# Seven block products for the q, k and v tiles of a hybrid SSD and DeltaNet block on one Trainium2 core

## The chip, the cores and the metric

The kernel is one launch on one core of a Trainium2 chip. The metric is the device time of that core in microseconds, the median of several executions of the same program. Engines are named as in the profile: PE is TensorE (PEld its weight loads), DVE is VectorE, ACT is ScalarE, POOL is GpSimd, SP is SyncE, which here only issues transfers.

## The reference, cut to what matters

Sequence and model width are both 1024, batch and depth 1, everything in float32.

```
h = rms_norm(x, g_mix_pre)
proj = h @ w_in                                  # 1024 x 1024 by 1024 x 8736
z, xbc, dt_raw, qkv, gate, b_raw, a_raw, m_gate = split(proj)
xbc = silu(causal_dwconv(xbc, conv_ssm_w) + conv_ssm_b)       # 1536 channels, 4 taps
qkv = silu(causal_dwconv(qkv, conv_gdn_w))                    # 3072 channels, 4 taps
y_ssm, y_gdn = chunked scans over xs, B, C and over q, k, v   # z and gate enter as silu(.)
x = x + rms_norm((gate_ssm * (y_ssm @ w_br_ssm) + gate_gdn * (y_gdn @ w_br_gdn)) @ w_out)
x = x + rms_norm((gelu(causal_dwconv(h @ w_ffn_gate) + b) * (h @ w_ffn_up)) @ w_ffn_down)
x = x + rms_norm(sigmoid(x @ w_ple_gate) * (p @ w_ple_proj))
```

The change concerns the products for `xbc` and `qkv` with their convolutions, and the stage behind them.

## The kernel before, in words

**Numbers in two parts.** Every matrix product is made of three in the fast float32 format of TensorE: a value is split in a high part (`act_hi`, `w_hi`) and the rest (`act_lo`, `w_lo`), and a product is hi x hi + lo x hi + hi x lo. The activations `h` lie on chip, channels on partitions: 8 blocks of 128 channels (`KD`) by 1024 tokens.

**Tiles.** A tile is 128 output channels by 1024 tokens. `pe_unit` (L488) makes a plain tile with `pe_steps` (L470): 8 blocks of input channels, two halves of 512 tokens, three matmuls each, so 48 matmuls of 128x512 into one of four PSUM buffers of two banks. A buffer is taken with `wait_buffer` and given back through `tile_free`. SP loads weights by 1 MB blocks of two tiles into one of two slots of `w_raw` (`load_block`, L428), GpSimd splits each tile's weights with two instructions of 128x1024 (`split_unit`, L465 and L467) into one of two slots of `w_hi` and `w_lo`; `unit_begun` tells it that TensorE has begun the unit before.

**The x, B, C, q, k and v tiles** (70 to 462 us) are 12 `ssm` tiles and 24 `gdn` tiles, in the order of the list `PROJ` (L370). For each, VectorE copies PSUM to `xin` (L2938), makes the first tap (L2945) and three more taps (L2951) into `ring_a`; ScalarE applies Silu into `ring_b` and sends the tile to the scratch tensor `spill` (L2856, L2859). Between tiles lie the head factors: `head_softplus` (L524) behind the twelfth tile, the transposes for `O_TM` behind the q and k tiles, the sums over tokens for `O_CUM` behind the first four v tiles, with `tm_sources`, `tm_sums` and four exponentials. Loops over four tiles (`run_tiles`) are hardware loops except for the first four tiles.

**The gates' stage** (462 to 731 us, functions with `_a`) makes 16 plain tiles for `z` and `gate` in 128 steps of six matmuls, in two PSUM buffers. Between the steps that `A_START` (L1152) and `A_AT` name, TensorE does the small work of the eight chunks of 128 tokens of the DeltaNet branch: `sums` (the sums of squares), `v_rows`, `gram` and `k_rows` in the other two buffers. For each chunk SP loads q, k and v back from `spill` (`qkv_load`, L1348), two broadcast decay arrays (`decays_load`, L1340) and a weight block, and stores seven results (`stores`, L1353). ScalarE makes squares, norms and exponentials (L1227 to L1245) and evicts the gate tiles (`evict`, L1218); VectorE scales q and k (L1290, L1292) and forms the matrices (L1300 to L1305), and from chunk 4 on solves blocks by substitution (`substitute`, L1402). GpSimd splits weights and prepares the decays (L1329, L1331).

**The FFN stage** (up to 2080 us) already makes a pair of tiles by seven block products (Strassen's scheme in Winograd's form): the 1024x1024 activations and the 1024x256 weights are cut in two by two blocks. Four sums of weight blocks come from VectorE (`sums`, L2404, L2416), the high parts from ScalarE (L2108), the low parts from GpSimd (L1755). A product (`product`, L1845) is 12 matmuls into one PSUM bank. ScalarE copies the first product out of PSUM (L2115) and VectorE adds up the two tiles with seven evictions (`evict`, L2418, L2434). The four sums of activation blocks are made once, with their high and low parts (L2397, L2078, L2402). There is one semaphore order for all engines, written out by hand.

## Time and profile before

| | |
|---|---|
| three runs, us | 2559.57, 2562.78, 2572.18 (median 2562.78) |
| the profiled execution, us | 2576.11 |
| its span, us | 2574.3 |
| busy us PE, PEld, DVE, ACT, POOL | 2468.0, 2041.2, 1542.1, 723.0, 1179.6 |
| mean granted clock of TensorE | 0.985 |

The span is the time from the first to the last instruction of the profiled execution. Busy times add up the instructions of an engine; a matmul's recorded length is longer than the distance to the next one, because matmuls are pipelined. A wait names the instruction whose end released the waiting engine.

### The profile page before, as it was taken

What the parts mean: (1) busy time and instruction counts of PE and PEld (TensorE: products, weight loads), DVE (VectorE), ACT (ScalarE), POOL (GpSimd) and SP (SyncE); (2) the same over time, 40 slices, a digit from 0 to 9 for tenths busy, and PEclk for the clock granted to TensorE, in tenths of its full rate; (3) what the DMA queues carried; (4) which work ended last, traced back from release to release, by engine and by line L of the source; (5) the groups of instructions that cost most, each with busy time, mean ns of one, the idle gap of its engine ahead of it and who ended that gap; (6) DMA issues with size and microseconds to landing.
All of it is one profiled execution on the core that took longest, in us unless ns stands there. A gap on an engine that the chain in (4) does not pass through costs nothing. (4 is left out here: it accounts for less than half of the span.)

```text
span 2574.3 us, 30045 instructions
## 1 busy us (share of the span) xinstructions
PE 2468.0 (96%) x11684; PEld 2041.2 (79%) x11684; DVE 1542.1 (60%) x1359; ACT 723.0 (28%) x830; POOL 1179.6 (46%) x631
## 2 busy tenths in 40 slices
PE   6999999999899999989999799999999999999998
PEld 5888888777678888878878578888888878888786
DVE  4679776435774667654243796776776752322585
ACT  4100101355412223232003353333333331000332
POOL 1333333456444545443334355655566543333563
PEclk7999999999999999999999899999999999999999
DMA  5222322688775756646232212222221253122332
GB/s 197 103 98 83 113 90 100 173 269 273 245 242 142 207 167 186 190 126 214 98 143 89 95 50 83 85 86 73 98 80 66 98 196 115 49 82 82 119 112 105
DMA packets 293583, 336.28 MB, mean 131 GB/s; under 512 B 44445, under 2 KB 250602, under 8 KB 289386
## 3 DMA queue, kind: packets, MB, share of 16 engines
q1 hardware_dynamic: 260634, 272.47, 33.2%
q10 hardware_dynamic: 32848, 62.40, 6.5%
q8 instruction: 71, 1.16, 0.2%
q14 instruction: 30, 0.25, 0.0%
HBM read 231.55 MB, written 103.28 MB: 130 GB/s over the span
## 5 line engine op out<-in xcount | busy, mean ns | idle before, releaser
L480 PE MATMUL ps<-act_hi,w_hi 128*128 128x512 f32 x1712 | 682.4, 399 | 14.8 <-POOL w_lo L467 4.5
L484 PE MATMUL ps<-act_hi,w_lo 128*128 128x512 f32 x1712 | 667.5, 390 | 0.0
L483 PE MATMUL ps<-act_lo,w_hi 128*128 128x512 f32 x1712 | 667.0, 390 | 0.0
L465 POOL TENSOR_SCALAR w_hi<-w_raw 128x1024 fp32r<-128x1024 f32 x151 | 171.7, 1137 | 914.8 <-issue 603.8
L467 POOL TENSOR_TENSOR w_lo<-w_raw,w_hi 128x1024 fp32r<-128x1024 f32 x151 | 409.2, 2710 | 12.6
L480 PEld LDWEIGHTS ps<-act_hi,w_hi 128*128 128x128 f32 x1712 | 322.2, 188 | 87.6 <-issue 11.6
L483 PEld LDWEIGHTS ps<-act_lo,w_hi 128*128 128x128 f32 x1712 | 322.3, 188 | 67.6 <-issue 3.6
L484 PEld LDWEIGHTS ps<-act_hi,w_lo 128*128 128x128 f32 x1712 | 321.8, 188 | 67.6
L1755 POOL TENSOR_TENSOR w_lo<-sm,w_hi 128x512 fp32r<-128x512 f32 x120 | 208.6, 1740 | 108.7 <-ACT w_hi L2108 108.7
L1755 POOL TENSOR_TENSOR w_lo<-w_raw,w_hi 128x512 fp32r<-128x512 f32 x90 | 138.8, 1543 | 164.5 <-ACT w_hi L2108 164.5
L2951 DVE SCALAR_TENSOR_TENSOR ring_a<-xin,par,ring_a 128x1024 f32<-128x1024 f32 x108 | 185.0, 1713 | 11.8 <-DVE ring_a L2945 0.3
L1870 PE MATMUL ps<-t,w_hi 128*128 128x512 f32 x480 | 186.8, 389 | 0.0
L1871 PE MATMUL ps<-t,w_hi 128*128 128x512 f32 x480 | 186.8, 389 | 0.0
L1872 PE MATMUL ps<-t,w_lo 128*128 128x512 f32 x480 | 186.7, 389 | 0.0
L1870 PE MATMUL ps<-act_hi,w_hi 128*128 128x512 f32 x360 | 140.9, 391 | 4.6 <-POOL w_lo L1755 4.6
L1872 PE MATMUL ps<-act_hi,w_lo 128*128 128x512 f32 x360 | 140.7, 391 | 0.0
L1871 PE MATMUL ps<-act_lo,w_hi 128*128 128x512 f32 x360 | 140.6, 391 | 0.0
L2856 ACT ACTIVATE ring_b<-ring_a 128x1024 f32<-128x1024 f32 x36 | 38.2, 1061 | 330.9 <-DVE ring_a L2951 330.9
L2517 DVE TENSOR_TENSOR tile<-ps,tile 128x1024 f32<-128x1024 f32 x24 | 29.4, 1224 | 160.8 <-PE ps L484 133.8
L2108 ACT ACTIVATE w_hi<-sm 128x512 fp32r<-128x512 f32 x120 | 75.4, 630 | 135.9 <-PE ps L1872 135.9
L1781 PE MATMUL ps<-act_hi,w_hi 128*128 128x512 f32 x256 | 103.1, 403 | 10.8 <-DVE act_lo L2360 7.1
L1870 PEld LDWEIGHTS ps<-t,w_hi 128*128 128x128 f32 x480 | 90.1, 188 | 18.8
(348 smaller groups left out, 4137.0 us busy)
## 6 DMA issues: line engine op xcount, KB each, us to landing
w_raw<-in_w_in_dram SPq DMA_DIRECT2D x34, 1024.0 KB, 5.2
spill<-ring_b ACTq DMA_DIRECT2D x67, 512.0 KB, 2.7
w_raw<-in_w_ffn_down_dram SPq DMA_DIRECT2D x18, 1024.0 KB, 4.8
w_raw<-in_w_ffn_up_dram SPq DMA_DIRECT2D x16, 1024.0 KB, 5.1
w_raw<-in_w_ffn_gate_dram SPq DMA_DIRECT2D x16, 1024.0 KB, 5.1
f_cm<-ring SPq DMA_DIRECT2D x32, 512.0 KB, 2.6
qkv_a<-spill SPq DMA_DIRECT2D x8, 1536.0 KB, 8.3
dec_a<-cum_rows SPq DMA_DIRECT2D x16, 512.0 KB, 14.3
```

The costliest lines, as they stand in the source:

```text
L465: nc.gpsimd.tensor_scalar(hi, raw, 1.0, 0.0, ALU.mult, ALU.add).then_inc(split_done, 1)
L467: nc.gpsimd.tensor_tensor(lo, raw, hi.bitcast(f32), ALU.subtract).then_inc(split_done, 1)
L480: first = nc.tensor.matmul(o, wh, mov[0][:, k, c], start=(k == 0), stop=False)
L483: nc.tensor.matmul(o, wh, mov[1][:, k, c], start=False, stop=False)
L484: last = nc.tensor.matmul(o, wl, mov[0][:, k, c], start=False, stop=(k == KD - 1))
L1755: nc.gpsimd.tensor_tensor(product_slot(w_lo, j), product_in(q, i), product_slot(w_hi, j).bitcast(f32), ALU.subtract).then_inc(w_low[0], 1)
L1781: first = nc.tensor.matmul(dst, wh, mov[0][:, k, in_half(half)], start=(k == 0), stop=False)
L1870: nc.tensor.matmul(dst, wh[:, k, :], mh[:, k, :], start=(k == 0), stop=False)
L1871: nc.tensor.matmul(dst, wh[:, k, :], ml[:, k, :], start=False, stop=False)
L1872: last = nc.tensor.matmul(dst, wl[:, k, :], mh[:, k, :], start=False, stop=(k == 3))
L2108: a(product_slot(w_hi, j), product_in(q, i), ACT.Copy).then_inc(w_high[0], 1)
L2951: v.scalar_tensor_tensor(out=ring_a[:, slot, :], in0=xin[:, slot, tap:tap + SEQ], scalar=col_of(wname, tap * nt + t0 + n), in1=ring_a[:, s ...
```

## The change

The 24 q, k and v tiles are made in twelve pairs by the seven block products of the FFN stage: `sp_pairs`, `pool_pairs`, `pe_pairs`, `act_pairs`, `dve_pairs` and `dve_sums` are new and written out, and `run_tiles` with its hardware loops is gone. VectorE makes the four weight sums of every pair. The four activation sums (`ct1` to `ct4`) are made by VectorE and ScalarE during the first twelve tiles. In all 36 tiles ScalarE makes the first tap, out of PSUM for the first twelve and from the assembled tile in the pairs, and Silu writes in place; the other three taps of the first twelve read PSUM, and the copy to `xin` is gone (`xin` and `ring_b` hold the assembled tiles of the pairs). The head work moves to between the first twelve tiles, and the eleven copies to `tmc` move with it. In the gates' stage `A_START` changes, SP's block requests move behind the loads of the chunk, and ScalarE's evictions move. GpSimd splits the first gate unit after the last pair's products. The diff, cut to its core:

```diff
-    A_START = [15, 27, 40, 55, 70, 85, 100, 116]
+    A_START = [22, 33, 45, 58, 72, 86, 101, 116]
...
+    IN_PRODUCTS = ("a11", "a12", "s1", "s2", "s4", "s3", "a22")
+    SUM_AT = {"s1": (0, 1), "s3": (3, 2), "s2": (1, 3), "s4": (2, 4)}
+    C_EVICT = {0: (1, 0), 1: (3, 0), 2: (2, 0), 3: (4, 0), 4: (5, 1), 5: (2, 1), 6: (6, 1)}
...
+    def pool_pairs(pool):
+        for p in range(C_PAIRS):
+            for i in range(PRODUCTS):
+                j = PRODUCTS * p + i
+                past(pool, c_high, j + 1)
+                nc.gpsimd.tensor_tensor(c_slot(w_lo, j), c_product_in(p, i), c_slot(w_hi, j).bitcast(f32),
+                                        ALU.subtract).then_inc(c_low[0], 1)
...
+    def pe_pairs(pe):
...
+        for p in range(C_PAIRS):
+            for i in range(PRODUCTS):
+                j = PRODUCTS * p + i
+                past(pe, c_low, j + 1)
...
+                elif p % 2:
+                    if i == 0 and p > 1:
+                        past(pe, c_copied, p - 1)
+                    if i == 1:
+                        past(pe, c_copied, p)
+                    if i in (2, 3):
+                        past(pe, c_evicted, SUMMED * (p - 1) + (1, 6)[i - 2])
+                elif i in (0, 1, 5):
+                    past(pe, c_evicted, SUMMED * (p - 1) + {0: 1, 1: 6, 5: 7}[i])
...
+                for k in range(4):
+                    first = nc.tensor.matmul(dst, wh[:, k, :], mh[:, k, :], start=(k == 0), stop=False)
...
+                    nc.tensor.matmul(dst, wh[:, k, :], ml[:, k, :], start=False, stop=False)
+                    last = nc.tensor.matmul(dst, wl[:, k, :], mh[:, k, :], start=False, stop=(k == 3))
+                last.then_inc(c_prod[0], 1)
+        pe.sem_inc(unit_begun, QKV_T - 1)
...
+        def first_tap(t):
+            past(act, c_evicted, SUMMED * (t // 2) + (4, 7)[t % 2])
+            act_first_tap(act, J_Q + t, c_tile(t), pcol("conv_gdn_w", 3 * QKV_T + t), None)
...
+        for p in range(C_PAIRS):
+            for i in range(PRODUCTS):
+                if p or i > 1:
+                    c_high_of(act, p, i)
+                if p and i == 0:
+                    first_tap(2 * p - 2)
+                if i == 3:
+                    copy(p)
+                    if p == 0:
+                        xbc_out(act, XBC_T - 1)
+                    if p > 1:
+                        silu(2 * p - 3)
+                if p and i == 4:
+                    first_tap(2 * p - 1)
+                if p and i == 6:
+                    silu(2 * p - 2)
...
+        for p in range(C_PAIRS):
+            evicts(p, (0,))
+            if p:
+                taps(2 * p - 2)
+            evicts(p, (1, 2))
+            if p < C_PAIRS - 1:
+                dve_sums(dve, p + 1)
+            evicts(p, (3, 4, 5))
+            if p:
+                taps(2 * p - 1)
+            evicts(p, (6,))
+        taps(QKV_T - 2)
+        taps(QKV_T - 1)
...
-        for m in range(2):
-            split_unit(pool, U_A, m)
+        past(pool, c_prod, PRODUCTS * C_PAIRS - 2)
+        pool.sem_inc(split_done, 2 * QKV_T)
+        split_unit(pool, U_A, 0)
+        past(pool, c_prod, PRODUCTS * C_PAIRS)
+        split_unit(pool, U_A, 1)
...
         for c in range(NCH):
-            if c:
-                block_load(c + 1)
             if c < NCH - 1:
                 decays_load(c + 1)
                 qkv_load(c + 1)
+            block_load(c + 2)
             if c == 4:
                 blocks_load(0)
-            if c == NCH - 1:
-                block_load(NCH + 1)
             stores(c)
...
+        after_norms = {0: 2, 2: 5, 5: 10, 6: 12, 7: 14}
+        after_decays = {1: 4, 3: 7, 4: 9}
+        after_squares = {0: 3, 2: 6, 3: 8, 5: 11, 6: 13, 7: 15}
...
+        conv(0)
+        head_softplus(dve, lambda step: conv({5: 1, 11: 2}[step]) if step in (5, 11) else None)
+        conv(3)
...
+        conv(10)
+        sum_low(ct4, ct4_raw, 4)
+        dve_sums(dve, 0)
+        conv(11)
+        dve_pairs(dve)
```

## Rows read from the trace of the kernel before

**Rows 1.** The header of the page.

```profile
span 2574.3 us, 30045 instructions
```

**Rows 2.** Stretches: length, busy us (instructions) of PE, PEld, DVE, ACT, POOL; PEclk, DMA, GB/s.

```profile
70.00:462.00 392.00, 392.00 (x1744) 323.49 (x1743) 301.24 (x199) 44.90 (x42) 137.11 (x70) 1.00 0.27 96
462.00:731.00 269.00, 257.04 (x1130) 202.75 (x1129) 132.53 (x143) 133.46 (x120) 140.91 (x68) 0.99 0.79 249
...
1600.00:1800.00 200.00, 200.00 (x884) 165.60 (x883) 139.78 (x147) 76.16 (x108) 120.05 (x75) 1.00 0.23 79
```

**Rows 3.** Timeline of TensorE near the end of the v tiles: start, us, instruction.

```profile
440.02 0.39 PE L480 MATMUL ps<-act_hi,w_hi 128*128 128x512 f32 x1
...
450.22 0.39 PE L480 MATMUL ps<-act_hi,w_hi 128*128 128x512 f32 x1
```

**Rows 4.** Waits of TensorE in the gates' stage: us in total, times, longest.

```profile
PE ps L1190 <- DVE hrow L1292: 7.3, 2, 5.4
PE ps L480 <- POOL w_lo L467: 2.6, 2, 1.3
PE ps L1170 <- ACT hrow L1232: 2.0, 1, 2.0
```

**Rows 5.** Groups of VectorE in the FFN stage: busy us, mean ns, idle before.

```profile
L2416 DVE TENSOR_TENSOR sm<-w_raw 128x512 f32<-128x512 f32 x54 | 49.1, 949 | 19.1 <-POOL w_lo L1755 19.1
L2447 DVE SCALAR_TENSOR_TENSOR fa<-xinb,par,fa 128x1024 f32<-128x1024 f32 x26 | 43.8, 1685 | 1.8
...
L2434 DVE TENSOR_TENSOR ring<-ps,sx 128x512 f32<-128x512 f32 x52 | 35.9, 691 | 19.6 <-PE ps L1872 18.3
...
L2416 DVE TENSOR_TENSOR sm<-sm,w_raw 128x512 f32<-128x512 f32 x27 | 32.7, 1210 | 0.0
```

**Rows 6.** Timelines of VectorE (160 us; FFN stage) and of GpSimd (FFN stage).

```profile
162.28 4.14 DVE L2951 SCALAR_TENSOR_TENSOR ring_a<-xin,par,ring_a 128x1024 f32<-128x1024 f32 x3
...
1679.78 3.50 DVE L2447 SCALAR_TENSOR_TENSOR fa<-xin,par,fa 128x1024 f32<-128x1024 f32 x2
...
1666.36 1.28 POOL L1755 TENSOR_TENSOR w_lo<-sm,w_hi 128x512 fp32r<-128x512 f32 x1 [0.89 <-ACT w_hi L2108]
...
1679.96 2.24 POOL L1755 TENSOR_TENSOR w_lo<-sm,w_hi 128x512 fp32r<-128x512 f32 x1 [0.81 <-ACT w_hi L2108]
```

**Rows 7.** A group of ScalarE in the FFN stage.

```profile
L2091 ACT ACTIVATE fa<-xinb,par 128x1024 f32<-128x1024 f32 x13 | 16.2, 1246 | 2.9 <-DVE xinb L2434 2.8
```

**Rows 8.** Groups of VectorE, 60 to 480 us; of line 2397 in the tail: min/median/max ns.

```profile
L2951 DVE SCALAR_TENSOR_TENSOR ring_a<-xin,par,ring_a 128x1024 f32<-128x1024 f32 x108 | 185.0, 1713 | 11.8 <-DVE ring_a L2945 0.3 <-DVE ring_a L2951 0.3
L2945 DVE TENSOR_SCALAR ring_a<-xin,par 128x1024 f32<-128x1024 f32 x36 | 48.2, 1338 | 6.7 <-DVE xin L2938 6.1 <-DVEq L2941 0.2
L2938 DVE COPY xin<-ps 128x1024 f32<-128x1024 f32 x36 | 44.0, 1222 | 78.9 <-PE ps L484 70.3 <-PE ps L2705 8.4 <-DVE hrow L546 0.2
...
L2397 DVE TENSOR_TENSOR t_raw<-res x2: 2282/2283/2284, 1483.0 to 1487.5; 128x2048 f32<-128x2048 f32 x2
```

**Rows 9.** Timeline of GpSimd at a split; of TensorE at 1064 us; a stretch after.

```profile
473.24 1.05 POOL L465 TENSOR_SCALAR w_hi<-w_raw 128x1024 fp32r<-128x1024 f32 x1 [6.99 <-issue]
474.37 2.39 POOL L467 TENSOR_TENSOR w_lo<-w_raw,w_hi 128x1024 fp32r<-128x1024 f32 x1
...
1063.97 1.97 PE L924 MATMUL ps<-ident,qs 128*128 128x128 f32 x8 [3.37 <-DVE qs L1126]
...
1065.00:1070.00 5.00, 5.00 (x30) 4.54 (x29) 5.00 (x5) 1.55 (x2) 0.68 (x1) 0.76 0.69 166
```

**Rows 10.** Timelines of ScalarE and TensorE in the gates' stage; landings of line 1351.

```profile
507.25 2.01 ACT L1232 ACTIVATE hrow<-qkv_a 128x1024 f32<-128x1024 f32 x2 [4.39 <-DMA qkv_a<-spill]
...
509.56 3.59 PE L1170 MATMUL ps<-hrow,ones 128*128 128x512 f32 x8
...
680.02 6.22 PE L1190 MATMUL ps<-hrow 128*128 128x256 f32 x16 [5.35 <-DVE hrow L1292]
...
DMA to landing us min/median/max: 7.0/8.3/13.7
```

More of the change, by code:

```diff
@@ L388, in uses_spilled @@
         return 16 * len(range(slot, j_end, 2))
-    def run_tiles(eng, tiles, j0, body):
-        if j0 == 0:
-            for n in range(tiles):
-                body(None, n)
-        else:
-            with eng.Fori(0, tiles // 4) as it:
-                for n in range(4):
-                    body(it, n)
     def uses(o0, n, it=None, per=0):
@@ L531, in then @@
             dve.wait_ge(head_dve, step[0])
+            between(step[0])
         dve.wait_ge(head_act, 2)
@@ L2622, in _ @@
             sp.dma_start(d_ch[64 * half:64 * half + 64, :], v.broadcast_to([64, KD]), allow_slow_non_contiguous=True).then_inc(d_in, 16)
[L2623 to L2629 removed]
+        for n in range(2, XBC_T, 2):
+            load_block(sp, w_in_k[:, :, COL_XBC + P * n:COL_XBC + P * n + 2 * P], 1, n // 2)
+        sp_pairs(sp)
         sp_a(sp)
@@ L2654, in _ @@
         split_unit(pool, U_SMALL, 0)
-        for kind, col, tiles, j0, o0 in PROJ:
-            run_tiles(pool, tiles, j0, lambda it, n: split_unit(pool, 1 + j0, n, it, 4))
+        for n in range(XBC_T):
+            split_unit(pool, 1, n)
+        pool_pairs(pool)
         pool_a(pool)
@@ L2871, in _ @@
+        act_pairs(act)
         act_a(act)
@@ new lines, in conv @@
+        def conv(n):
+            past(dve, c_first, n + 1)
+            o = xbc_use(n)
+            b, c = uses(o, 0)
+            src, out = buf(b), ring_a[:, n % 2, :]
+            for i, back in enumerate((1, 2, 3)):
+                if i:
+                    dve.wait_ge(conv_step, 2 * n + i)
+                v.scalar_tensor_tensor(out=out[:, back:SEQ], in0=src[:, 0:SEQ - back], scalar=pcol("conv_ssm_w", (3 - back) * XBC_T + n),
+                                       in1=out[:, back:SEQ], op0=ALU.mult, op1=ALU.add
+                                       ).then_inc(conv_step if i < 2 else tile_free[b], 1)
+            if n == 0:
+                dve.wait_ge(tile_free[b], c + 1)
+                v.sem_inc(tile_free[b], UNUSED[b])
@@ new lines, in _ @@
+        raw_op(ct2_raw, ct2_raw[:, :, :], ct1_raw[:, :, :], ALU.subtract)
+        conv(5)
+        past(dve, c_traw, 5)
+        sum_low(ct1, ct1_raw, 1)
+        conv(6)
+        tm_sums(dve)
+        conv(7)
+        dve.wait_ge(tm_act, 4)
+        for at, i, row, n in TM_COLS:
+            v.tensor_copy(tmc[:, :, at:at + n], tmh[:, :, i, row:row + n]).then_inc(tm_kept, 1)
+        dve.wait_ge(tm_kept, len(TM_COLS))
+        dve.wait_ge(cum_kept, 16)
+        raw_op(ct3_raw, ct2_raw[:, :, :], part(act_hi, 0, 0), ALU.subtract)
```

407 lines of the change are left out of this document (277 added, 130 removed).

## The prediction

> **What bounds the kernel now.** Read the header of the page first: the span is 2574.3 us [rows 1]. Then the busy time by stretch. From 70 to 462 us, the stage that this change rewrites, TensorE is busy in all 392.00 us at full granted clock, VectorE in 301 us and GpSimd in 137 us; in the gates' stage (462 to 731 us) TensorE idles 12 us; in the FFN stage, which runs seven block products for each pair of tiles already, it is busy in all of 200 us with VectorE at 140 us [rows 2]. A busy TensorE is worth its instruction rate: from the timeline, 45 matmuls start between 440.02 and 450.22 us, one each 0.2267 us [rows 3]. So a plain tile (48 matmuls) takes 10.88 us and 24 q, k and v tiles take 261.1 us. The path is TensorE, and fewer matmuls shorten it only if nothing else becomes the slower engine. The waits of TensorE in the gates' stage are few: 7.3 us on VectorE before `gram`, 2.6 us on GpSimd's weight split, 2.0 us on ScalarE's squares [rows 4].
>
> **Fewer matmuls.** A pair takes 7 products of 12 matmuls, 84 instead of 96, at 0.2267 us: 19.04 us a pair, 228.5 us for twelve. That is 144 matmuls less: **-32.6 us**, certain as work, not as time.
>
> **VectorE in a pair.** It now does 7 evictions of 128x512 out of PSUM, 4 weight sums of 128x512 and 6 filter taps of 128x1024 in each 19.04 us. By the means of the FFN stage [rows 5]: 7 x 0.69 = 4.8; sums 2 x 0.949 + 1.210 + about 1.2 = 4.3; 6 x 1.685 = 10.1; together 19.2 us, and some 0.04 us between each two of 17 instructions makes 19.9. That is already more than TensorE's 19.04. The FFN stage does two pairs with 14 evictions, 8 sums, 4 taps and 2 products in 38 us and has 30% of VectorE free; here a pair has three times the taps, and nothing is free. Those means hide a contention. Three taps alone take 4.14 us (1.38 each), but two taps beside a GpSimd instruction take 3.50 us, and the GpSimd instruction that needs 1.28 us by itself takes 2.24 us when it begins 0.18 us after a tap [rows 6]: GpSimd ends about 1.15 us after the tap did, and the second tap 1.1 us after GpSimd. The two take turns. A PSUM eviction keeps its 0.69 us. Bounds: with no turn lost VectorE needs 7 x 0.72 + 4 x 0.62 + 6 x 1.38 = 15.9 us (sums at 0.62 by the undisturbed ones, an estimate from 0.69 less the start-up shared by two in a row), so TensorE's 19.04 sets the pair; with all seven GpSimd subtractions of a pair in VectorE's way it needs 15.9 + 7 x 1.15 = 24.0 us. A busy VectorE spends a quarter of its time in evictions, which collide with nothing, so 5 of 7 collide, at 0.9 us each (part of a start-up is hidden): 15.9 + 4.5 = **20.4 us a pair**, nearest to the row sum of 19.9. Where it shows: VectorE's fourth eviction of a pair completes an early tile, ScalarE's first tap waits for it, ScalarE's copy of the next pair's second weight block stands behind that tap in its queue, GpSimd's subtraction behind that, and TensorE's second product of the next pair waits, 1.4 us per pair. The first two pairs run on the lead that exists. So 10 x 1.36 = **+13.6 us** given back (0 to +30; at the full 24.0 the change loses).
>
> The shared port is also a rule of the Trainium skill: "SBUF — State Buffer", section "SBUF: two separate sides", says that a VectorE instruction with two SBUF inputs and a GpSimd instruction exclude each other for a whole instruction, the loser waiting fully. By it the taps and sums (6 x 1.1 + 4 x 0.55 us) and the subtractions (7 x 1.15 us) hold the port 16.9 us of a 19.04 us pair, so the port alone does not bound the pair; rows 6 agree with the turns it describes.
>
> **ScalarE and GpSimd in a pair.** ScalarE: two first taps of 1.25 us [rows 7], eight copies of half that size at half that, two Silu at no more than 1.25: 10 us of 19.04. GpSimd: 7 subtractions of 1.3 to 1.7, at most 12 us. Both are hidden, and so are the 1 MB block loads, requested a pair ahead as in the FFN stage. If VectorE's lag grows, the cover of ScalarE's 1.25 us tap is what goes first.
>
> **The first twelve tiles.** VectorE loses the 1.22 us PSUM copy and the 1.34 us first tap of each [rows 8], and its taps now read PSUM with one SBUF input, so about 3.8 us a tile instead of 7.7. It gains nine 128x2048 sums and differences of the activations and four more for their low parts, 13 x 2.3 = 30 us [rows 8]. The head work, which stood partly among the q, k and v tiles, is 301 us less 36 tiles of 1.22 + 1.34 + 3 x 1.71 = 7.7 us [rows 2, 8], so 24 us. With 46 us of taps and 4 us of weight sums VectorE has 104 us of work beside 130 us of TensorE. Its queue order has about 2.5 us of room where tile 6 and tile 7 need their buffers back. I take **+1 us** (0 to +6). The transposes and cumulative sums on TensorE only change places.
>
> **From pairs to gates.** GpSimd may split the first gate unit only after the products of the last pair, because it waits for `unit_begun` to reach 37 and TensorE adds the missing 23 after its last product. The split is 1.05 + 2.39 us [rows 9] and stood during a tile before; VectorE's overdue taps can stretch it by two turns of about 1.1. TensorE stands still 3.5 us (2.9 to 5.5). After a stop of 3.37 us the granted clock fell below 2.4 GHz: 0.76 over the next 5 us [rows 9], 0.24 x 5 = 1.2 us lost. **+5 us** in all.
>
> **The gates' stage.** `A_START[0]` goes from step 15 to 22 (a step is 6 matmuls, 1.36 us): the last tiles finish later (VectorE has up to three tiles' taps left, 12 us; then Silu, store and a 1.5 MB load of about 9 us), some 26 us against 22 x 1.36 = 29.9 us. The 2.0 us wait on the squares goes. SP's block request moves from ahead of the decay and q/k/v loads to behind them and ahead of the stores of the preceding chunk: weights arrive a chunk earlier, so the two GpSimd waits (2.6 us) go. Behind it in SP's queue stand seven stores; its own wait, for the split of the chunk's units, is met by then. The q/k/v load no longer has the decay loads in front. But the next chunk's sums start one step sooner for chunks 1 and 2, and there was no room: the load let the squares run from 507.25 to 509.26 us, and the sums began at 509.56 [rows 10]. I take back 1 us. The 5.35 us stop before `gram` at 680.02 [rows 10] stays: the steps from `k_rows(5)` to `gram(6)` are 12 as before, and VectorE's substitution fills them. Sum: -2.0 - 2.6 + 1 + 0.6 for chunk 5, which begins a step sooner after chunk 4: **-3 us** (-11, all stops gone, to +8).
>
> Sum: -32.6 + 13.6 + 1 + 5 - 3 = **-16.0 us**. The profiled execution took 2576.1 us (span and 1.8 us around it), 13.3 us above the median of 2562.8; both should move alike, to 2560 and **2547 us**.
>
> **Rivals.**
> 1. Full cover: VectorE's turns fall into its evictions, a pair takes 19.04 us. For: the FFN stage shows no TensorE stop at all. Against: 19.9 us by its own means. 2562.8 - 29.6 = 2533 us.
> 2. VectorE bound harder: a spill that lands late holds ScalarE's second tap too, or the stops drop the clock. A pair of 21.6 us adds 12 us: 2559 us, no measurable change.
> 3. Slower than before: the 1 MB block that SP now requests beside each 1.5 MB q/k/v load delays it. The landings of that load lie between 7.0 and 13.7 us, median 8.3 [rows 10]; 13.7 for seven chunks is 7 x 5.4 = 38 us with no room to hide it: 2547 + 38 = 2585 us. It decides from 16 / 7 = 2.3 us a chunk on. Against: the block is requested after the load.
> That the change does not do what it says is excluded for the matmuls, which are written out.
>
> **Numbers.** Forecast case 0.42 (its own range 2540 to 2555), rival 1 0.22, rival 2 0.26, rival 3 0.10. A measurement here tells about 0.5%, 12.8 us, from no change. Faster by more than that (under 2550.0): all of rival 1, three quarters of the forecast, little of rival 2, 0.53. Within it: the rest of both and nearly all of rival 2, 0.38. Slower: most of rival 3, 0.09. The range leaves out only rival 3 and the far end of rival 1: 2527 to 2567 us.
>
> **What would show it.** A pair of products about 20.4 us long, with a wait of TensorE on GpSimd's subtraction near 1.4 us at the second product, and VectorE over 95% busy from the third pair on. Taps near 1.8 us in the pairs and 1.25 us on PSUM. One stop of 3 to 5 us between pairs and gates, with a dip of the clock. No wait on the weight split inside the gates' stage, and the 5 us stop before `gram` of chunk 6 still there. Wrong if VectorE has clear idle time in the pairs, or if sums in the gates' stage wait on q/k/v loads.

## The result, and the profile after

| | median us | runs | lowest to highest | profiled execution, span |
|---|---|---|---|---|
| before | 2570.74 | 12 | 2559.57 to 2577.61 | 2576.11, 2574.3 |
| after | 2577.33 | 12 | 2571.73 to 2580.71 | 2578.95, 2577.2 |

The ratio is 1.003 with an interval of 1.0016 to 1.0045: some 7 us slower, within the 0.5% that the prediction called no change, where 16 us less was forecast. The prediction started from three runs of the kernel before (median 2562.78); twelve runs have 2570.74, so 8 us of the distance to its 2547 us lie in that starting point and not in the change. First, the stretches of the kernel after, as in [rows 2]: the first line ends where the pairs end, the second is the gates' stage, the third the FFN stage, whose cost did not change.

```profile
70.00:433.00 363.00, 359.83 (x1590) 293.73 (x1589) 330.74 (x278) 143.17 (x174) 185.71 (x105) 1.00 0.29 100
433.00:726.00 293.00, 260.66 (x1093) 202.06 (x1092) 128.56 (x137) 129.56 (x118) 132.29 (x67) 0.94 0.71 223
1600.00:1800.00 200.00, 200.00 (x884) 165.62 (x883) 138.90 (x146) 76.07 (x107) 118.43 (x73) 1.00 0.24 83
```

The pairs paid: TensorE comes to the gates' units at 432.55 us, where it came at about 461.8 before (its first sums fell due at step 15 at 482.2 us, less 15 x 1.36). That is 29 us ahead. The last store of the gates' stage is requested at 726.32 us, before at 723.09. So this stage went from 261.3 to 293.8 us: **32 us lost where 3 were to be gained**. TensorE idles 32 us in it, against 12, and the granted clock is 0.94 in place of 0.99: some 20 us of the loss are idle time, and the other 12 fit the lower clock (0.05 of 293 us is 15 us, an estimate). The waits of TensorE in that stretch (us in total, times, longest) stand against [rows 4]; a stop, below, is one such wait:

```profile
PE ps L1414 <- ACT hrow L1478: 13.2, 4, 4.0
PE ps L494 <- POOL w_lo L481: 11.1, 2, 7.9
PE ps L1434 <- DVE hrow L1539: 7.9, 2, 4.3
```

The first line is the sums waiting for the squares (2.0 us before), the second the split of gate weights (2.6 us before, forecast to go), the third `gram`. In the pairs, VectorE's groups from 225 to 425 us (busy us, mean ns, idle before):

```profile
L719 DVE SCALAR_TENSOR_TENSOR ring_a<-xin,par,ring_a 128x1023 f32<-128x1023 f32 (+2 forms) x33 | 57.8, 1751 | 0.8
L719 DVE SCALAR_TENSOR_TENSOR ring_a<-ring_b,par,ring_a 128x1023 f32<-128x1023 f32 (+2 forms) x30 | 52.1, 1737 | 0.7
L692 DVE TENSOR_TENSOR csm<-w_raw 128x512 f32<-128x512 f32 x20 | 31.8, 1630 | 0.0
L711 DVE TENSOR_TENSOR ring_b<-ps,csx 128x512 f32<-128x512 f32 x21 | 14.4, 684 | 5.1 <-PE ps L599 4.7
```

VectorE is busy in 197.47 of those 200 us: it bounds the pairs, as forecast (e4 below tests it). And the timeline of TensorE gives the length of a pair, from the second product of one to the second product of the next, 377.07 - 357.55 = 19.52 us:

```profile
357.55 0.50 PE L595 MATMUL ps<-act_hi,w_hi 128*128 128x512 f32 x1 [0.17 <-POOL w_lo L563]
377.07 0.50 PE L595 MATMUL ps<-act_hi,w_hi 128*128 128x512 f32 x1 [0.18 <-POOL w_lo L563]
```

**Where the gates' stage lost it.** The timeline at its head, chunk 0 (ScalarE's squares, TensorE's sums, GpSimd, then the stop):

```profile
464.57 2.00 ACT L1478 ACTIVATE hrow<-qkv_a 128x1024 f32<-128x1024 f32 x2 [8.96 <-DMA qkv_a<-spill]
465.88 5.37 PE L1414 MATMUL ps<-hrow,ones 128*128 128x512 f32 x8 [3.23 <-ACT hrow L1478]
...
469.33 1.89 POOL L1579 TENSOR_TENSOR dec_a<-dec_a,tmc 128x1024 f32<-128x1024 f32 x1 [20.11 <-issue]
...
473.66 1.06 POOL L479 TENSOR_SCALAR w_hi<-w_raw 128x1024 fp32r<-128x1024 f32 x1
...
474.80 2.34 POOL L481 TENSOR_TENSOR w_lo<-w_raw,w_hi 128x1024 fp32r<-128x1024 f32 x1
...
477.29 0.77 PE L494 MATMUL ps<-act_hi,w_hi 128*128 128x512 f32 x1 [3.29 <-POOL w_lo L481]
...
479.98 1.37 PE L1422 MATMUL ps<-ident,qkv_a 128*128 128x128 f32 x8
```

GpSimd stood still 20.11 us in front of the decay work of chunk 0, and the split of unit `U_A+3` stood behind that in its queue. The unit is due at step 24. With the first sums at step 22 that is between the sums and the v rows (`L1422`), so the stop of 3.29 us delays the chunk too; with the sums at step 15 the v rows were already done. The sums themselves and the matmuls behind the stop ran at a lower clock: 5.37 us for the sums that took 3.59 us in [rows 10], and 0.77 us for a matmul of 0.39 us, which is the lower of the clock's two levels (1.2 and 2.4 GHz). Next, SyncE's requests and GpSimd's split of the block that came next:

```profile
487.75 0.36 SPq L1606 DMA_DIRECT2D qkv_a<-spill  x1
488.16 4.07 SPq L451 DMA_DIRECT2D w_raw<-in_w_in_dram  x1
```

```profile
498.63 1.04 POOL L479 TENSOR_SCALAR w_hi<-w_raw 128x1024 fp32r<-128x1024 f32 x1 [11.99 <-DMA w_raw<-in_w_in_dram]
...
502.25 0.77 PE L494 MATMUL ps<-act_hi,w_hi 128*128 128x512 f32 x1 [7.85 <-POOL w_lo L481]
```

Block 2 went out behind the second q, k and v load, 33 us behind the first, and TensorE needed it at 494.4 us.

**The view that explains the stage is the chain of its chunks.** The q, k and v load of chunk c+1 overwrites what VectorE reads last in chunk c (`L1539`). So a chunk is: load, squares, sums, norms, v rows, VectorE's last read, next load; eight of them in a row. A period is the time from one load's request to the next. From the timelines of SyncE, the request of the first and the eighth such load and of the last store of the stage (us), with each kernel's ratio to before:

| kernel | load 0 | load 7 | seven periods | last store | ratio, interval |
|---|---|---|---|---|---|
| before | 473.98 | 680.00 | 206.0 | 723.09 | 1 |
| after | 454.67 | 685.46 | 230.8 | 726.32 | 1.0030, 1.0016 to 1.0045 |
| e3 | 461.54 | 675.33 | 213.8 | 716.22 | 0.9989, 0.9974 to 1.0003 |
| e2 | 454.62 | 670.98 | 216.4 | 713.83 | 0.9969, 0.9953 to 0.9986 |
| e14 | 454.92 | 669.11 | 214.2 | 710.99 | 0.9962, 0.9949 to 0.9974 |
| e15 | 454.95 | 667.30 | 212.4 | 709.19 | 0.9956, 0.9939 to 0.9972 |
| e4 | 441.00 | 667.85 | 226.9 | 709.72 | 0.9954, 0.9940 to 0.9968 |
| e7 | 462.51 | 671.73 | 209.2 | 713.79 | 0.9949, 0.9934 to 0.9964 |
| e5 | 455.09 | 658.45 | 203.4 | 699.65 | 0.9938, 0.9914 to 0.9962 |
| e19 | 452.73 | 663.70 | 211.0 | 706.76 | 0.9934, 0.9916 to 0.9952 |
| e16 | 455.26 | 658.49 | 203.2 | 698.58 | 0.9923, 0.9907 to 0.9940 |
| e13 | 455.98 | 655.74 | 199.8 | 697.87 | 0.9916, 0.9888 to 0.9943 |
| e18 | 452.02 | 653.47 | 201.4 | 697.52 | 0.9911, 0.9894 to 0.9928 |
| e17 | 452.22 | 656.34 | 204.1 | 696.91 | 0.9908, 0.9887 to 0.9928 |
| e20 | 453.89 | 654.79 | 200.9 | 696.07 | 0.9898, 0.9881 to 0.9915 |
| e12 | 441.43 | 651.19 | 209.8 | 694.62 | 0.9878, 0.9848 to 0.9909 |

From the eighth load to the last store it is 40.1 to 44.1 us in every one, so the stage ends when the chain ends. TensorE's steps are links of the chain too: its sums and v rows stand behind the gate units that come first in its order. In the kernel before, the sums waited for the squares in chunk 0 alone (2.05 us), but there was little room: in chunks 1 to 6 they began 1.9 to 5.2 us behind the start of the squares, and 1.3 us is the least in any chunk (507.25 and 509.56 us in chunk 1, [rows 10]). Steps and chain were of nearly one length. In the kernel after, the sums waited for the squares in chunks 0, 3, 4 and 5, and `gram` for VectorE in chunks 5 and 6. After the change TensorE arrives 29 us sooner, the chain only 19 us (454.67 against 473.98), and then five of the seven periods took longer: 33.1, 34.8, 25.2, 30.2, 31.8, 39.2, 36.5 us after, against 25.6, 26.4, 25.9, 32.5, 29.4, 31.4, 34.8 before.

### The profile page after: what moved, and what is told of

Same layout as the page of the kernel before. It is cut to its first block and busy times, and to the rows that moved or that the text cites. A ratio compares the mean times of both kernels' runs of the same rounds, so it can differ in the third digit from the quotient of the medians.

```text
span 2577.2 us, 29644 instructions
## 1 busy us (share of the span) xinstructions
PE 2451.5 (95%) x11540; PEld 2019.9 (78%) x11540; DVE 1567.1 (61%) x1432; ACT 819.0 (32%) x961; POOL 1225.2 (48%) x667
## 5 line engine op out<-in xcount | busy, mean ns | idle before, releaser
L494 PE MATMUL ps<-act_hi,w_hi 128*128 128x512 f32 x1328 | 533.6, 402 | 24.7 <-POOL w_lo L481 13.0
L498 PE MATMUL ps<-act_hi,w_lo 128*128 128x512 f32 x1328 | 519.7, 391 | 0.0
L497 PE MATMUL ps<-act_lo,w_hi 128*128 128x512 f32 x1328 | 519.2, 391 | 0.0
L479 POOL TENSOR_SCALAR w_hi<-w_raw 128x1024 fp32r<-128x1024 f32 x127 | 146.2, 1151 | 752.6 <-issue 630.7
L481 POOL TENSOR_TENSOR w_lo<-w_raw,w_hi 128x1024 fp32r<-128x1024 f32 x127 | 343.2, 2702 | 10.6
L494 PEld LDWEIGHTS ps<-act_hi,w_hi 128*128 128x128 f32 x1328 | 250.7, 189 | 84.1 <-issue 19.9
L498 PEld LDWEIGHTS ps<-act_hi,w_lo 128*128 128x128 f32 x1328 | 250.5, 189 | 53.2
L497 PEld LDWEIGHTS ps<-act_lo,w_hi 128*128 128x128 f32 x1328 | 250.9, 189 | 52.2 <-issue 3.3
L2111 PE MATMUL ps<-act_hi,w_hi 128*128 128x512 f32 x360 | 141.2, 392 | 4.2 <-POOL w_lo L1996 4.2
L2112 PE MATMUL ps<-act_lo,w_hi 128*128 128x512 f32 x360 | 141.0, 392 | 0.0
L2113 PE MATMUL ps<-act_hi,w_lo 128*128 128x512 f32 x360 | 141.0, 392 | 0.0
L2758 DVE TENSOR_TENSOR tile<-ps,tile 128x1024 f32<-128x1024 f32 x24 | 29.4, 1224 | 160.8 <-PE ps L498 133.8
L2022 PE MATMUL ps<-act_hi,w_hi 128*128 128x512 f32 x256 | 103.1, 403 | 10.4 <-DVE act_lo L2601 6.8
L2423 ACT ACTIVATE act_hi<-f_raw 128x1024 fp32r<-128x1024 f32 x32 | 31.2, 1047 | 254.9 <-DMA f_raw<-f_cm 254.9
L563 POOL TENSOR_TENSOR w_lo<-csm,w_hi 128x512 fp32r<-128x512 f32 x48 | 84.7, 1774 | 43.4 <-ACT w_hi L631 43.4
```

Of the source, the lines that this page charges most:

```text
L479: nc.gpsimd.tensor_scalar(hi, raw, 1.0, 0.0, ALU.mult, ALU.add).then_inc(split_done, 1)
L481: nc.gpsimd.tensor_tensor(lo, raw, hi.bitcast(f32), ALU.subtract).then_inc(split_done, 1)
L494: first = nc.tensor.matmul(o, wh, mov[0][:, k, c], start=(k == 0), stop=False)
L497: nc.tensor.matmul(o, wh, mov[1][:, k, c], start=False, stop=False)
L498: last = nc.tensor.matmul(o, wl, mov[0][:, k, c], start=False, stop=(k == KD - 1))
L563: nc.gpsimd.tensor_tensor(c_slot(w_lo, j), c_product_in(p, i), c_slot(w_hi, j).bitcast(f32), ALU.subtract).then_inc(c_low[0], 1)
```

## The experiments

Diffs are against the kernel named; a us figure between two of them is the difference of their ratios times 2571. An interval reaches 3 to 8 us to either side, so where two overlap the text says so. Three theories at first: A, the chain starts late because the last tiles do; B, requests at the head of the stage are late; C, the re-ordering itself.

**e3, two requests early.** The load of block 2 is then left out of the loop's first turn.

```diff
+        past(sp, c_prod, PRODUCTS * C_PAIRS)
+        decays_load(0)
+        block_load(2)
         for k in range(2):
             sp.wait_ge(spilled[k], uses_spilled(J_Z, k))
         qkv_load(0)
-        decays_load(0)
```

> The change, with two of SP's requests at the head of the gates' stage moved: decays_load(0) and block_load(2) go out as soon as the last pair product is done (about 433 us), ahead of the waits for the last spills. After the change they were requested at 455.1 and 488.2 us. Theory B (the lost time of the gates' stage comes from late requests at its head): ScalarE's copy and GpSimd's half of unit U_A+3 no longer stand behind a late decay load, so TensorE's stop of 3.29 us at 477.29 goes, and block 2 is there 50 us sooner, so the stop of 7.85 us at 502.25 goes, and with them some of the lost clock (0.93 and less in the slices after them): 11 to 16 us less than the change, 2561 to 2566 us. Theory A (the chain of chunks starts late because VectorE and ScalarE finish the last q, k and v tiles late): the two stops go, but TensorE then runs into the next waits for squares and gram sooner, so that most of it comes back as longer stops at 562, 594, 626 and 649 us: under 4 us gained.

Both stops on the split went, and the kernel took 10 us less than the change: nearer to B, a little short of its 11 to 16. But a new stop of 5.92 us came at 460.37 us, on ScalarE's eviction of a gate tile, and the first q, k and v load went out 7 us later. ScalarE's first tap of tile 23 waits for the spill of tile 21; beside the early loads that spill took 12.90 us. The timeline of ScalarE in e3, and the same wait in the kernel after:

```profile
439.76 0.33 ACTq L617 DMA_DIRECT2D spill<-ring_a  x1
452.64 1.15 ACT L608 ACTIVATE ring_a<-ring_b,par 128x1024 f32<-128x1024 f32 x1 [12.90 <-DMA spill<-ring_a]
```

```profile
442.51 1.15 ACT L608 ACTIVATE ring_a<-ring_b,par 128x1024 f32<-128x1024 f32 x1 [2.73 <-DMA spill<-ring_a]
```

A store of 0.5 MB on the critical chain lost 10 us to a weight block and decay rows that could have waited. In e7, which has the same early requests, the wait was 12.02 us.

**e4, no VectorE backlog.**

```diff
-  v.scalar_tensor_tensor(out=out[:, back:SEQ], in0=src[:, 0:SEQ - back], ..., in1=out[:, back:SEQ], ...)
+  v.scalar_tensor_tensor(out=out[:, back:back + 16], in0=src[:, 0:16], ..., in1=out[:, back:back + 16], ...)
```

> The change, with VectorE's three filter taps of each of the 24 q, k and v tiles done for the first 16 tokens only (the filters of these tiles are left out beyond that; 72 instructions shrink from about 1.5 us to 0.1 us). VectorE loses about 100 us of work in the pairs' stage and has nothing overdue at its end. Theory A (late last tiles start the chunk chain late): Silu of tile 23 comes at about 437 instead of 450 us, the first q, k and v load at about 441 instead of 454.7, the wait of the first sums for squares (3.23 us at 465.9) goes, and the later chunks have 10 us more room, so the waits for squares and gram in the gates' stage fall from 21 us to under 8, 12 us or more gained there; the pairs take 19.04 us instead of 19.5, 5 us more. In all 2555 to 2562 us. Theory B (late requests of the decays and of block 2, and the order of the eight chunks): the chain starts sooner, but block 2 still goes out behind the second q, k and v load and lands late, and the sums and grams from chunk 3 on wait as before: 5 us from the pairs and 3 us from the first sums, about 2569 us.

19.5 us less than the change, 2560.69 us, in A's range. Twelve pairs took 228.5 us (201.5 to 430.0), 19.04 each, with no wait on `L563` at all: VectorE was the bound. The first load went out at 441.00. But 25 us of waits stayed in the gates' stage, 18 of them for squares and before `gram`, not under 8, and its seven periods were nearly as bad as the change's (226.9 us against 230.8). So lateness and slow periods are two losses.

**e5, the gates' stage as before.** SyncE's order (the block of the next units a chunk later, behind the stores of the chunk before), the start steps and ScalarE's order of evictions are those of the kernel before; the short form of the edit:

```diff
-    A_START = [22, 33, 45, 58, 72, 86, 101, 116]
+    A_START = [15, 27, 40, 55, 70, 85, 100, 116]
...
+            if c:
+                block_load(c + 1)
             if c < NCH - 1:
                 decays_load(c + 1)
                 qkv_load(c + 1)
-            block_load(c + 2)
```

> The twelve pairs stay as in the change, but the gates' stage is put back: SP's order of requests, A_START and ScalarE's order of evictions are those of the kernel before. Theory C (the re-ordering itself costs the gates' stage its 32 us): the stage falls back to about 260 us after the pairs, and the kernel takes about 2545 to 2550 us. Theory A (the chain of chunks starts late against TensorE, 9 us later than before, whatever the order): the first sums, now at step 15, wait about 10 us for the first load and its squares, and nothing is gained over the change, 2572 to 2580 us, in many stops of other places.

24 us less than the change, 16 less than before: C, though its 2555.02 us are 5 above C's range, with A's residue, a stop of 10.18 us at the first sums, and little else. Timeline and waits of TensorE in e5:

```profile
463.73 5.80 PE L1414 MATMUL ps<-hrow,ones 128*128 128x512 f32 x8 [10.18 <-ACT hrow L1478]
```

```profile
PE ps L1414 <- ACT hrow L1478: 13.0, 2, 10.2
PE ps L494 <- POOL w_lo L481: 2.7, 2, 1.4
```

The profiled execution of e5 is the fastest of its six (2543.1 against a median of 2555.0); its stage is as in e13 and e17, what follows (span less last store) took 4 to 12 us less than in the other traces here.

**e7, blocks ahead of the other loads.** e3 with `if c: block_load(c + 2)` moved to the top of the loop.

> As e3_early_loads, and in the loop over chunks the block of the next units is requested ahead of the decay and q, k and v loads of the next chunk instead of behind them. If a block that lands late and splits that wait for it are the cause of the stops at 623 and 700 us, one or two us less than e3_early_loads; if the q, k and v loads are what is late (landings of 13.9 and 15.4 us with a block beside them), those loads start with 1 MB in front of them, land some 3 us later each, and TensorE's waits for squares grow: 5 to 15 us slower than e3_early_loads.

Both expectations missed: 10 us less than e3 by the ratios. Its trace shows only 2.4 us of that in this stage (last store 713.79 against 716.22); 5 us lie behind it, unexplained. The feared cost of a block ahead of the q, k and v load is not there (landings have a median of 9.1 us, 10.7 in e3): the block goes out while that load still waits for VectorE's last read, at 528.39 us before the load at 547.64, for one.

**e2, start steps and evictions of before, SyncE's new order.** Only the first line of e5's diff, and ScalarE's order.

> The change with A_START and ScalarE's order of evictions put back as before, but SP's new order of requests kept: against e5_old_gates it has one thing more, the block of the next units requested behind the q, k and v load instead of a chunk later behind the stores. If the start steps and the eviction order are what cost the gates' stage 24 us (TensorE's chunk work sits too close together, 94 steps from the first to the last chunk instead of 101): within 4 us of e5_old_gates, ratio 0.993 to 0.995. If the 1 MB block beside the 1.5 MB q, k and v load costs it (rival 3: landings of 13.9 and 15.4 us): the stage stays slow, ratio 1.000 to 1.003.

In between. By the ratios start steps and evictions cost 16 us (after to e2) and SyncE's order another 8 us (e2 to e5, intervals overlapping); by the last stores of the traces it is 12 and 14 us. So the share of each is not settled, only the 24 us of both. Slow landings of the q, k and v load do not tell e2 from e5. They (request to landing, min/median/max) are no shorter without the block behind them; first the kernel after, then e5 (e2 has 7.4/9.8/15.1):

```profile
DMA to landing us min/median/max: 7.2/9.3/15.6
```

```profile
DMA to landing us min/median/max: 7.3/11.3/17.2
```

What differs is chunks 5 and 6, where in e2 VectorE's last read came 14.2 and 13.2 us behind the start of the v rows, in e5 4.6 and 6.9: its substitution work had slipped beside GpSimd's splits (from 620.70 us three steps of it in e2 take 2.46, 1.93 and 2.43 us; e16 tests this). TensorE in e2, waiting for that read:

```profile
634.50 5.47 PE L1434 MATMUL ps<-hrow 128*128 128x256 f32 x16 [6.43 <-DVE hrow L1535]
...
671.01 5.99 PE L1434 MATMUL ps<-hrow 128*128 128x256 f32 x16 [5.36 <-DVE hrow L1535]
```

Start steps and evictions are hard to part further. With the new order of evictions `evict(1)` stands ahead of the squares and waits for a unit that ends with step 15, so the sums can't be due at step 15; with the old one `evict(2)` stands behind the norms of chunk 1, whose sums are due at step 33, while TensorE needs it at step 32. Either way the queues would wait for each other in a ring (read from the kernels, not run).

**e14, SyncE's order alone.**

```diff
         for c in range(NCH):
+            block_load(c + 2)
             if c < NCH - 1:
                 decays_load(c + 1)
                 qkv_load(c + 1)
-            block_load(c + 2)
```

> The change with one thing moved: in each chunk SP requests the block of the next units ahead of the decay and q, k and v loads of the next chunk, so block 2 goes out at about 471 us instead of 488.2, while nothing else is being loaded; start steps and evictions are those of the change. If the order of requests is the cause (B): no stop of 7.85 us on the weight split at 502, landings of the q, k and v load back at 8 to 9 us, 10 to 16 us faster than the change, ratio 0.997 to 0.999. If the start steps are the cause: the 7.85 us stop goes and turns into waits for squares and gram in later chunks, ratio 1.001 to 1.003.

17.5 us less than the change, all of B's gain: the 7.85 us stop went, and the second period fell from 34.8 to 23.1 us. The landings did not go back to 8 to 9 us as expected (7.2/9.3/16.2). SyncE's order alone is worth more here than the 8 us between e2 and e5: the shares depend on what else is in place. The split of `U_A+3` still waited behind the decays. GpSimd and TensorE in e14:

```profile
470.38 1.89 POOL L1579 TENSOR_TENSOR dec_a<-dec_a,tmc 128x1024 f32<-128x1024 f32 x1 [20.94 <-issue]
...
478.32 0.76 PE L494 MATMUL ps<-act_hi,w_hi 128*128 128x512 f32 x1 [3.75 <-POOL w_lo L481]
```

**e12, e5 with the short taps of e4.**

> e5_old_gates with VectorE's three taps of the 24 q, k and v tiles done for the first 16 tokens only (the filters beyond them are left out). It asks what the late last tiles cost once the gates' stage has its old order. Theory A2 (TensorE's stop of 10.2 us at the first sums is VectorE's backlog from the pairs): Silu of tile 23 some 12 us sooner, the stop shrinks to under 1 us, the clock stays up behind it, and with pairs of 19.04 us the kernel takes 14 to 18 us less than e5_old_gates, ratio 0.987 to 0.989. Rival (the gates' stage is bound by the chain of its chunks elsewhere): the stop goes but other stops grow, under 8 us less than e5_old_gates.

A2 (the stop is VectorE's backlog from the pairs): 15 us less than e5, and the stop of 10.18 us became 0.60 us. The traces alone show less: the first load went out 13.7 us sooner, but the seven periods took 209.8 us in place of 203.4, so that the last store came only 5 us sooner (e5's quick profiled execution hides the rest, or the stage gave back a part, as the rival had it). It leaves the filters out, so it is a bound and no version: what VectorE's load in the pairs still costs.

**e13, first steps 17 and 28** (`A_START = [17, 28, 40, 55, 70, 85, 100, 116]` in e5).

> e5_old_gates with the first two start steps at 17 and 28 instead of 15 and 27. TensorE fills 2 steps, 2.7 us, of its 10.2 us stop before the first sums with unit matmuls. If that stop is plain waiting: 2.7 us less than e5_old_gates, hardly more than the interval; if the later chunks are what bounds the stage (second chunk 11 steps behind the first instead of 12), nothing changes.

The stop fell from 10.18 to 7.64 us, as expected; the ratios (0.9938 and 0.9916) are not apart by their intervals.

**e15, the split ahead of the decays,** e14 with GpSimd's two splits together:

```diff
-            if m < 2:
-                split_unit(pool, U_A, m + 2)
+            if m == 0:
+                split_unit(pool, U_A, 2)
+                split_unit(pool, U_A, 3)
```

> e14_block_first with one step of GpSimd's queue moved: the split of unit U_A+3 stands ahead of the first decay work of chunk 0, not behind it. In e14_block_first the split waited for the decay load (landed about 470 us) and TensorE stopped 3.75 us on it at 478.3 us, between the sums and the v rows of chunk 0, which made the first period of the chunk chain (from one q, k and v load to the next) 34.2 us instead of 26.4. Theory D (the gates' stage is a serial chain of chunk loads, and what delays one period delays the end): the first period falls to 27 to 29 us, the last chunk ends 5 to 7 us sooner, ratio 0.9935 to 0.9945. Rival (the time comes back in a later period, as landings of 14 to 16 us do now): under 2 us, ratio 0.9955 or more.

The first period fell as said, from 34.2 to 25.7 us, and the second rose from 23.1 to 29.9: the rival (ratios 0.9956 and 0.9962, intervals overlapping). In that period it took 13.3 us from the load's request to the squares instead of 8.2. The load had been asked for 8 us sooner, closer behind block 2 and the decays; that these were still under way is likely and not shown.

**e16, the substitution spread.**

```diff
-                substitute(dve, 0, (0, 26, 52, SUB_STEPS)[c - 4:c - 2])
+                substitute(dve, 0, ((0, 18), (26, 40), (48, SUB_STEPS))[c - 4])
...
+            if c in (5, 6):
+                substitute(dve, 0, ((18, 26), (40, 48))[c - 5])
             for batch in range(2):
```

> e15_split_ahead with VectorE's substitution spread: of the 26 steps between chunks 5 and 6 and the 26 between 4 and 5, eight each go into the gap ahead of the gram products of the next chunk. In the new order VectorE's last read of q, k and v came 10.5 and 12.1 us after the v rows in chunks 5 and 6 instead of 4.6, because substitution steps of 2.4 us beside GpSimd stood in front. Theory D: the periods of chunks 5 and 6 fall from 34 to about 30 us each, 5 to 8 us less than e15_split_ahead. Rival (the chain of these chunks is bound elsewhere, by landings or by gram): within 2 us of e15_split_ahead.

8.5 us less than e15 (the intervals just touch), and the last store 10.6 us sooner: D, that what delays one period delays the end. What was moved shows in VectorE's and GpSimd's timelines of e14, where the eviction of the v rows (TensorE had them at 624.9 us) stands behind it:

```profile
622.53 0.37 DVE L1679 TENSOR_TENSOR sub_d<-sub_d,xin 128x198 f32<-128x198 f32 x1
622.93 1.10 DVE L1676 TENSOR_TENSOR xin<-sub_n,sub_d 128x210 f32<-128x210 f32 x1
624.07 2.44 DVE L1679 TENSOR_TENSOR sub_d<-sub_d,xin 128x210 f32<-128x210 f32 x1
626.55 1.97 DVE L1676 TENSOR_TENSOR xin<-sub_n,sub_d 128x220 f32<-128x220 f32 x1
628.55 2.46 DVE L1679 TENSOR_TENSOR sub_d<-sub_d,xin 128x220 f32<-128x220 f32 x1
...
631.91 1.22 DVE L1533 TENSOR_TENSOR ring_a<-ps,tmc 128x1024 f32<-128x1024 f32 x1
```

```profile
622.72 1.10 POOL L479 TENSOR_SCALAR w_hi<-w_raw 128x1024 fp32r<-128x1024 f32 x1 [11.81 <-issue]
623.90 2.38 POOL L481 TENSOR_TENSOR w_lo<-w_raw,w_hi 128x1024 fp32r<-128x1024 f32 x1
626.25 2.03 POOL L1579 TENSOR_TENSOR dec_a<-dec_a,tmc 128x1024 f32<-128x1024 f32 x1
628.35 2.42 POOL L1581 TENSOR_TENSOR dec_a<-dec_a,m_incl 128x1024 f32<-128x1024 f32 x1
```

Steps of 0.4 us take 2.0 to 2.5 us while GpSimd splits a weight and prepares the decays, each about as long as the GpSimd instruction beside it. In e5 every step of the same piece took 0.2 to 0.4 us, clear of the splits.

**e17, e13 with both splits ahead and behind the last tap** (`pool.wait_ge(conv_step, 2 * XBC_T + 3 * QKV_T)` ahead of them).

> e13_start17 with GpSimd's splits of units U_A+2 and U_A+3 both ahead of the decays of chunk 0, and the first of them behind the last filter tap. In e13_start17 that split lay beside the last three taps (about 6.6 us instead of 3.9). Theory A2: the last tile is ready 2.7 us sooner, the first q, k and v load goes out 2.7 us sooner, and TensorE's stop at the first sums falls from 7.6 to about 5 us; 2 to 4 us less than e13_start17, ratio 0.990 to 0.991. Rival: the two splits now end so late that TensorE waits at step 16, no gain, ratio 0.9916.

As expected in each step, with ratios that are not apart (0.9908 against 0.9916 in e13): last three taps 3.92 us instead of 6.61, load 0 at 452.22, stop 5.21 us. VectorE and TensorE in e17:

```profile
443.91 3.92 DVE L719 SCALAR_TENSOR_TENSOR ring_a<-ring_b,par,ring_a 128x1023 f32<-128x1023 f32 x3 [0.57 <-ACT ring_a L608]
```

```profile
461.28 5.17 PE L1414 MATMUL ps<-hrow,ones 128*128 128x512 f32 x8 [5.21 <-ACT hrow L1478]
...
503.07 0.77 PE L494 MATMUL ps<-act_hi,w_hi 128*128 128x512 f32 x1 [5.02 <-POOL w_lo L481]
```

**e18, e17 with the spread of e16.**

> e17_start17_split with the substitution spread as in e16_split_spread. With the old order of requests the last read of q, k and v came only 5 to 6 us after the v rows in every chunk, so Theory D expects nothing here: within 2 us of e17_start17_split. If the spread steps collide with GpSimd ahead of gram, 2 to 6 us more.

Within the interval of e17: nothing, as expected.

**e19, e17 with e14's order; e20, e19 with the spread.**

> e17_start17_split with the block of the next units requested ahead of the decay and q, k and v loads of the next chunk, as in e14_block_first. In e17_start17_split block 2 was still requested behind the stores of chunk 0, and TensorE stopped 5.0 us on its split at 503.1 us with the granted clock at 0.86 in the slice around it. Theory E (early block requests are good in themselves, and cost the change only where they stand behind the q, k and v load): that stop goes, 5 to 8 us less than e17_start17_split, ratio 0.988 to 0.989. Rival (any block that is not the last request of a chunk puts 1 MB beside the q, k and v load or in front of it: landings go up by some 3 us in most chunks): 0 to 6 us more than e17_start17_split, ratio 0.991 to 0.993.

> e19_start17_block_first with VectorE's substitution spread as in e16_split_spread. If with this order of requests VectorE's last read of q, k and v again comes 10 to 12 us behind the v rows in chunks 5 and 6 (as in e14 and e15), the spread gives 5 to 7 us as it did in e16_split_spread; if the start steps of before keep substitution clear of GpSimd's splits (as in e13 and e17), nothing within 2 us.

e19: the stop on block 2 went, yet the last store came 9.9 us later than in e17 (ratio 0.9934 against 0.9908, intervals overlapping). Not by landings, as the rival had it (median 10.1 us, 11.1 in e17): in chunks 5 and 6 VectorE's last read came 11.0 and 13.1 us behind the v rows, the substitution beside GpSimd again. e20, which removes that, takes 9 us less than e19: **0.9898 (0.9881 to 0.9915), 2542.47 us, the lowest ratio of a complete kernel here, 1.0% under before and 1.3% under the change**. e17 and e18 have intervals that overlap its own. What TensorE still waits for in its gates' stage:

```profile
PE ps L1414 <- ACT hrow L1478: 10.2, 3, 5.0
PE ps L494 <- ACT ring_b L1469: 1.5, 1, 1.5
```

## Why the prediction was wrong

- **Fewer matmuls, -32.6:** right.
- **VectorE in a pair, 20.4 us, +13.6:** the mechanism was right (98.7% busy; e4 gives 19.04), the size was not. The wait sat where it was forecast, on GpSimd's subtraction at the second product, in eight pairs, but with 0.2 us in the record and 0.48 us lost by a pair in all, instead of 1.4, and a pair took 19.52 us: 8 x 0.48 = **+3.8** (200.18 to 432.55 us is 232.4, against 228.5). The step that was mis-sized is the 0.9 us for each of five collisions, on top of bounds that add up to 15.8 us and not 15.9; taps of 1.74 us, evictions of 0.68 us and sums of 0.7 to 1.6 us make 19.9 us for the 17 instructions of a pair, a little more than the pair itself, since their recorded lengths overlap. The row sum of 19.9 us had been the better guide.
- **First tiles, +1:** a wait of 1.8 us at 126 us, and nothing net by 432.55 us.
- **Pairs to gates, +5:** nothing. The step that failed is that the first split may begin only after the last pair's products, as the description of the change has it too. GpSimd waits for 82 of the 84 products and for an increment behind the last one in TensorE's queue, and its split began 4 us ahead of the last product's end (below).
- **Gates' stage, -3 (-11 to +8):** +32. This is the term that turned the result, and the step that failed. It read `A_START` as steps of TensorE with room to spare ("some 26 us against 22 x 1.36"), and priced SyncE's move by what it removes. What it left out is that each chunk's load waits for VectorE's last read of the chunk before, so the stage is a chain of eight periods; the working looked at waits of TensorE (12 us in all, [rows 4]) and took them for all that could change in the stage. The runs show in its place: 24 us from start steps, evictions and SyncE's order together (e5), and the rest from the chain starting late against TensorE (5 us in e5's stage, 699.65 - 433 against 261.3; how much of it an undelayed chain would win back is open, from 3 us by e12's trace, whose stage is 694.62 - 430.47 us long, to 13 by its ratio, whose 15 us hold 3 of the pairs). How the 24 us divide depends on the order in which the edits are undone: 16 and 8 by way of e2, 17.5 for SyncE's order alone in e14.
- **The lateness** was in the working (12 us of taps, then Silu, store, load), but with no turns lost to GpSimd. The squares came 32 us behind the first unit, not 26. The load took 9.9 us, near the "about 9" of the working; the excess is in the taps, which ended 18 us behind the first unit (Silu of the last tile begins at 450.33 us), the last three of them in 6.60 us beside GpSimd's split.
- **Rival 3** (slower than before) had the sign of the stage right and its mechanism at most in part. Landings rose from a median of 8.3 to 9.3 us, not to 13.7. The median hides two chunks: from request to squares, chunks 4 and 5 took 15.4 and 15.7 us after against 9.0 and 7.8 before, and in chunks 3 to 5 TensorE's sums waited 9.9 us for squares. But the block behind the load is not shown as the cause: e5 goes without it, has a median of 11.3 us and took 12.9, 14.5 and 17.2 us in chunks 4 to 6, and its seven periods are 27 us shorter in all. The moved request did cost something else: block 2 came behind the load of chunk 1, where TensorE waited 7.85 us for it (e14, block first: 17.5 us less), and the substitution slipped beside the splits (e2 against e5).
- **Rivals 1 and 2** did not come: the pair lies between them.
- **What would show it:** the condition "wrong if sums in the gates' stage wait on q/k/v loads" was met four times. So was the failure of another sign, "no wait on the weight split": there were 11.1 us of it. The 5 us stop before `gram` of chunk 6 stayed (4.27 us at 685.48).

Left open: how the 24 us divide among start steps, evictions and SyncE's order (no kernel with start steps or evictions alone ran), why the profiled executions of before and after differ by 3 us where the medians differ by 7, what slows the q, k and v loads of the middle chunks, and why e5's profiled execution was 4 to 12 us quicker behind this stage than the others.

## What to carry to other kernels

Where a stage holds work in rounds that reload one buffer, write down the round's chain from request to last read on every queue, and ask of a change what it does to the chain's start and to each period; the idle time of the busiest engine hides this as long as both are of one length. A start step is a promise about another engine: moved later, it can put due work of other units between two links of the chain, as the unit of step 24 came between the sums and the v rows here. Of a request that is moved, ask when its own user needs it (block 2 was 8 us late), and keep bulk loads away from a store that the chain is waiting for. And keep VectorE's filler work with two SBUF inputs away from the moments when GpSimd works: here a step of 0.4 us took up to 2.5.

## What the runs showed of the hardware that was not expected

**A semaphore increment of TensorE's queue runs ahead of its matmuls.** `pe.sem_inc` stands behind the last product in program order. GpSimd's split needs that increment, since no product after the first raises the same count. Its timeline after the change shows it released by TensorE's sequencer (PEq) at about 428.7 us, while the last matmul of the pairs begins at 432.32:

```profile
428.73 1.05 POOL L479 TENSOR_SCALAR w_hi<-w_raw 128x1024 fp32r<-128x1024 f32 x1 [1.00 <-PEq L601]
```

```profile
432.32 0.39 PE L599 MATMUL ps<-ct,w_lo 128*128 128x512 f32 x1
```

That is some 16 matmuls; in e17 the split began at 428.95 us in the same way. It is why the forecast stop of 5 us did not exist: the split was done before the products were. The order is safe here only since the split also waits for a count that products raise when they end (the 82nd; the last two read the other slot). The Trainium skill, "Perfetto Trace Analysis", section "Tensor Engine Instruction (MATMUL, LD_WEIGHTS)", says that the sequencer is free for its next instruction once a matmul has been pushed to the wait queue; the trace agrees, with 3.6 us of lead.

**A small store beside transfers in flight took over four times as long**: ScalarE waited 2.73 us for the 0.5 MB spill of tile 21 in the kernel after, 12.90 us in e3 and 12.02 us in e7, where a 1 MB weight block and the decay rows had been requested shortly before it.

**VectorE against GpSimd**: 0.4 us steps of the substitution took 1.97 to 2.47 us beside GpSimd's instructions of 128x1024 (e14, e19), a loss of 1.6 to 2.1 us each, where the prediction had priced a turn at 0.9. The Trainium skill, "SBUF — State Buffer", section "SBUF: two separate sides", has the loser wait for the whole instruction of the other; the trace agrees, since a 2.4 us step is about one GpSimd subtraction long (2.38 us), and a long instruction paid as much as a short one: in e17 a tap of 128x1021 took 3.29 us at 435.62 us, where three clear of GpSimd took 3.92 us in all.
